# First stage of a two-block transformer kernel: the first value tile moved ahead of modulation tiles 8 and 9, and the tokens' sums of squares moved from VectorE to TensorE

## What is computed

```python
sc_lat, sc_ctx = jax.nn.silu(c), jax.nn.silu(c_ctx)
m_l = (sc_lat @ w_ada[l] + b_ada[l])[:, None, :]
m_c = sc_ctx @ w_ada[l] + b_ada[l]
sh1, sc1, g1, sh2, sc2, g2 = jnp.split(m_l, 6, axis=-1)
csh1, csc1, cg1, csh2, csc2, cg2 = jnp.split(m_c, 6, axis=-1)
hl = modulate(rmsnorm(lat, norm_g[l, 0]), sh1, sc1)
hc = modulate(rmsnorm(cx, norm_g[l, 0]), csh1, csc1)
...
q, zf_fwd, zf_bwd, v, g = jnp.split(h @ w_in, 5, axis=-1)
```

## Time and profile before

| | |
|---|---|
| median of three executions | 931.19 us |
| the profiled execution | 931.22 us, with a span of 929.4 us |
| TensorE (PE) busy | 908.6 us, 98% |
| VectorE (DVE) busy | 647.0 us, 70% |
| ScalarE (ACT) busy | 507.7 us, 55% |
| granted TensorE clock, mean | 0.994 of full speed |
| chain of waits, by engine | PE 91%, DVE 4%, DMA 1%, ACT 1%, issue 1%, SPq 1% |

### The profile page before, as it was taken

How to read it: one execution, slowest core, us unless ns; L and a number is a source line. 1 busy time by engine, 2 the same in 40 slices (tenths; PEclk the granted TensorE clock), 3 DMA queues, 4 the chain that set the end, 5 groups by cost and what they waited for, 6 DMA issues and landing times.

```text
span 929.4 us, 17184 instructions
## 1 busy us (share of the span) xinstructions
PE 908.6 (98%) x6354; PEld 830.5 (89%) x6354; DVE 647.0 (70%) x1054; ACT 507.7 (55%) x798; POOL 0.2 (0%) x4
## 2 busy tenths in 40 slices
PE   7899999999999999999999999999999999999997
PEld 5468888888899999999998998999999899999996
DVE  5978488888887777676677866774466766555555
ACT  6642466666664665555556655544464565444443
POOL 0000000000000000000000000000000000000000
PEclk9899999999999999999999999999999999999999
DMA  9829553443425265655654443344445446555551
GB/s 346 322 104 348 222 191 136 137 135 135 132 95 181 70 210 177 202 176 169 198 182 157 133 159 120 134 173 154 169 146 202 157 159 222 185 181 181 188 185 57
DMA packets 45343, 160.94 MB, mean 173 GB/s; under 512 B 5104, under 2 KB 6512, under 8 KB 45168
## 3 DMA queue, kind: packets, MB, share of 16 engines
q1 hardware_dynamic: 43536, 156.56, 48.8%
q10 hardware_dynamic: 1760, 3.74, 1.1%
HBM read 159.23 MB, written 1.05 MB: 172 GB/s over the span
## 4 chain that ended last, share of the span: by engine, by line
PE 91%; DVE 4%; DMA 1%; ACT 1%; issue 1%; SPq 1%; DVEq 0%; ACTq 0%
PE bank L438 22%; PE bank L440 21%; PE bank L439 21%; PE bank L1166 4%; PE bank L504 4%; PE bank L505 4%; PE bank L506 4%; DMA arena<-in_stream 1%; DVE w_lo L432 1%; PE bank L1227 1%; PE bank L1269 1%; PE bank L1249 1%; PE bank L1265 1%; PE bank L1199 1%; PE bank L1229 1%
## 5 line engine op out<-in xcount | busy, mean ns | idle before, releaser
L432 DVE TENSOR_TENSOR w_lo<-raw,w_hi 128x1024 fp32r<-128x1024 f32 x248 | 299.7, 1222 | 143.5 <-ACT w_hi L421 143.2
L438 PE MATMUL bank<-h_hi,w_hi 128*128 128x256 f32 (+1 forms) x1248 | 373.9, 300 | 1.9 <-DVE h_lo L620 0.6
L440 PE MATMUL bank<-h_hi,w_lo 128*128 128x256 f32 (+1 forms) x1248 | 366.6, 294 | 0.0
L439 PE MATMUL bank<-h_lo,w_hi 128*128 128x256 f32 (+1 forms) x1248 | 365.9, 293 | 0.0
L421 ACT ACTIVATE w_hi<-raw 128x1024 fp32r<-128x1024 f32 x248 | 257.4, 1051 | 99.0 <-PE bank L440 76.8
L438 PEld LDWEIGHTS bank<-h_hi,w_hi 128*128 128x128 f32 x1248 | 234.6, 188 | 12.1 <-issue 3.6
L439 PEld LDWEIGHTS bank<-h_lo,w_hi 128*128 128x128 f32 x1248 | 236.2, 189 | 6.3
L440 PEld LDWEIGHTS bank<-h_hi,w_lo 128*128 128x128 f32 x1248 | 234.7, 188 | 5.9
L438 PE MATMUL bank<-y_hi,w_hi 128*128 128x256 f32 x304 | 86.9, 286 | 0.0
L440 PE MATMUL bank<-y_hi,w_lo 128*128 128x256 f32 x304 | 85.9, 282 | 0.0
L439 PE MATMUL bank<-y_lo,w_hi 128*128 128x256 f32 x304 | 85.4, 281 | 0.0
(11 more groups left out here) (255 smaller groups left out, 1138.1 us busy)
## 6 DMA issues: line engine op xcount, KB each, us to landing
raw<-in_stream SPq DMA_DIRECT2D x248, 512.0 KB, 3.3
arena<-in_ada SPq DMA_DIRECT2D x24, 512.0 KB, 5.3
arena<-in_stream SPq DMA_DIRECT2D x6, 1024.0 KB, 14.3
xres<-in_ada SPq DMA_DIRECT2D x8, 512.0 KB, 3.2
tok<-in_tok SPq DMA_DIRECT2D x4, 512.0 KB, 9.0
con<-in_con ACTq DMA_DIRECT2D x1, 1472.0 KB, 9.5
xres<-in_tok ACTq DMA_DIRECT2D x1, 1024.0 KB, 9.8
out<-arena SPq DMA_DIRECT2D x4, 256.0 KB, 2.0
```

The lines of the kernel that those rows point to most:

```text
L432: dve.tensor_tensor(w_lo[c.slot][:, :], source(c), w_hi[c.slot][:, :].bitcast(F32), ALU.subtract).then_inc(S("split_lo"), 1)
L438: pe.matmul(dst, hi_w, a_hi, start=start, stop=False, skip_group_check=True)
L439: pe.matmul(dst, hi_w, a_lo, start=False, stop=False, skip_group_check=True)
L440: return pe.matmul(dst, lo_w, a_hi, start=False, stop=stop, skip_group_check=True)
```

## The change

On TensorE, value tile 0 becomes chunk 8, directly behind modulation tiles 0 to 7, and modulation tiles 8 to 15 follow it. The seven additions on VectorE and the one product with ones are gone. In their place TensorE multiplies each tile of squares with the matrix of ones itself: eight products that add up in bank 1, two each behind modulation tiles 2, 3, 5 and 7 (`PIECE_BEHIND`). The zero products behind tiles 0 to 3 and 9 are gone (25 of them), and 10 stand ahead of value tile 0 (`FILL`). Loads, ScalarE's and VectorE's instructions are put in an order that goes with this. The core of the diff:

```diff
-TOPPED = (5, 5, 5, 4, 0, 0, 0, 0, 0, 6)
+FILL = 10
+PIECE_BEHIND = (2, 3, 5, 7)
-V_FIRST = KT + AHEAD
+V_FIRST = KT
...
             for i in range(KT):
                 ada(i)
-                warm(TOPPED[i])
-                if i == 3:
-                    pe.wait_ge(S("tok_added"), KT - 1)
-                    pe.matmul(psum[1][:, :], ones, wide[:, 0:TC], start=True, stop=True).then_inc(S("tok_summed"), 1)
+                if i in PIECE_BEHIND:
+                    n = PIECE_BEHIND.index(i)
+                    pe.wait_ge(S("tok_squares"), n + 1)
+                    for k in range(2 * n, 2 * n + 2):
+                        last = pe.matmul(psum[1][:, :], ones, wide[:, k * TC:(k + 1) * TC], start=k == 0, stop=k == KT - 1)
+                    if n == 3:
+                        last.then_inc(S("tok_summed"), 1)
                 if i == 5:
                     turn_rows(0)
             turn_rows(1)
+            warm(FILL)
...
             lo(dve, Chunk(4))
             lo(dve, Chunk(5))
+            quarter(0)
+            lo(dve, Chunk(6))
+            lo(dve, Chunk(7))
+            lo(dve, Chunk(V_FIRST))
+            quarter(1)
             norm_tokens(0)
             norm_tokens(1)
-            lo(dve, Chunk(6))
-            quarter(0)
-            norm_tokens(2)
...
             split_tokens(0)
-            lo(dve, Chunk(V_FIRST))
             split_tokens(1)
             lo(dve, Chunk(V_FIRST + 1))
+            norm_tokens(2)
+            norm_tokens(3)
+            lo(dve, Chunk(V_FIRST + 2))
+            split_tokens(2)
+            lo(dve, Chunk(V_FIRST + 3))
+            split_tokens(3)
             for k in range(4, KT):
                 norm_tokens(k)
-            split_tokens(2)
-            lo(dve, Chunk(V_FIRST + 2))
-            split_tokens(3)
-            for n in range(V_FIRST + 3, EARLY):
+            for n in range(V_FIRST + 4, EARLY):
                 lo(dve, Chunk(n))
             quarter(2)
```

More of the change, by code:

```diff
@@ L118 @@
 WARM = 12
-TOPPED = (5, 5, 5, 4, 0, 0, 0, 0, 0, 6)
-SKIPPED = (4, 3, 2, 3)
+FILL = 10
+PIECE_BEHIND = (2, 3, 5, 7)
+SKIPPED = 3
 E_QD, E_QE, E_KE, E_KD = 1, 4, 5, 6
@@ L417, in hi @@
             else:
-                act.wait_ge(S(f"loaded{c.slot}"), c.round * 16 + (16 - 16 * SKIPPED[c.slot]))
+                act.wait_ge(S(f"loaded{c.slot}"), c.round * 16 + (16 - 16 * SKIPPED))
             if n >= RING:
@@ L699, in load_stream @@
                     load(stream_in, i * (RING * P) + u * P, u)
[L701 to L709, removed]
             def load_ada(pair):
@@ L714, in load_ada, with load_tokens @@
                              stream_in[first:first + 2 * P, :].rearrange("(c p) n -> p c n", p=P)).then_inc(S(f"ada_in{pair}"), 16)
+            def load_tokens(n):
+                x = slice(n * 2 * TC, (n + 1) * 2 * TC)
+                sp.dma_start(tok[:, x], tok_in[:, x]).then_inc(S(f"tok_in{n}"), 16)
             def load_one(n, split):
@@ L718, in load_one @@
                 load(stream_in, n * P, n % RING)
[L720 to L723, removed]
+            sp.dma_start(cc[:, :], cc_in).then_inc(S("cc_in"), 16)
+            load(stream_in, 0, 0)
+            sp.dma_start(con[:, 0:2 * P], con_in[:, 0:2 * P]).then_inc(S("con_in"), 16)
+            load(stream_in, P, 1)
+            load(stream_in, 2 * P, 2)
+            load_tokens(0)
+            load(stream_in, 3 * P, 3)
+            load_tokens(1)
+            sp.dma_start(par[:, :], par_in).then_inc(S("par_in"), 16)
+            load_ada(0)
+            load_tokens(2)
+            load_ada(1)
+            load_tokens(3)
+            load_one(V_FIRST, 1)
+            for pair in range(2, KT - RING // 2):
                 load_ada(pair)
@@ L732, in load_mods @@
                     sp.dma_start(mod_raw[slot], ada_in[n * P:(n + 1) * P, :]).then_inc(S(f"mod_loaded{slot}"), 16)
-            for n, split in ((EARLY, 2), (EARLY + 1, V_FIRST + 1), (EARLY + 2, 4)):
+            for n, split in ((EARLY, 2), (EARLY + 1, 3), (EARLY + 2, 4)):
                 load_one(n, split)
+            sp.wait_ge(S("split_lo"), V_FIRST + 3)
             load_mods(0)
@@ L789, in modulate, with square_pieces @@
                     act.activation(x, x, ACT.Identity, scale=gain[:, k:k + 1], bias=shift[:, k:k + 1]).then_inc(S("modulated"), 1)
-            for n in range(6):
-                hi(act, Chunk(n))
[L793 to L796, removed]
-            copy_rows(0)
+            def square_pieces(n):
+                x = slice(n * 2 * TC, (n + 1) * 2 * TC)
+                act.wait_ge(S(f"tok_in{n}"), 16)
+                act.activation(wide[:, x], tok[:, x], ACT.Square).then_inc(S("tok_squares"), 1)
+            for n in range(3):
+                hi(act, Chunk(n))
+            square_pieces(0)
+            hi(act, Chunk(3))
+            square_pieces(1)
+            hi(act, Chunk(4))
+            hi(act, Chunk(5))
+            copy_rows(0)
+            square_pieces(2)
+            hi(act, Chunk(6))
+            hi(act, Chunk(7))
+            square_pieces(3)
+            act.wait_ge(S("lb_diff"), 1)
+            act.activation(lb_d, lb_d, ACT.Exp).then_inc(S("lb_exp"), 1)
+            hi(act, Chunk(V_FIRST))
+            copy_rows(1)
             act.wait_ge(S("tok_summed"), 1)
@@ L802, in _ @@
             act.activation(rstd, rstd, ACT.Exp, scale=-0.5).then_inc(S("tok_rstd"), 1)
[L803 to L809, removed]
             modulate(0)
-            hi(act, Chunk(V_FIRST))
             modulate(1)
             hi(act, Chunk(V_FIRST + 1))
+            hi(act, Chunk(V_FIRST + 2))
             modulate(2)
-            hi(act, Chunk(V_FIRST + 2))
+            hi(act, Chunk(V_FIRST + 3))
             modulate(3)
-            for n in range(V_FIRST + 3, EARLY):
+            for n in range(V_FIRST + 4, EARLY):
                 hi(act, Chunk(n))
@@ L1610, in split_tokens @@
                 dve.tensor_tensor(h_lo[:, x], tok[:, x], h_hi[:, x].bitcast(F32), ALU.subtract).then_inc(S("h_lo"), 2)
[L1612 to L1619, removed]
             for n in range(4):
                 lo(dve, Chunk(n))
-                add_token_squares(n)
             dve.wait_ge(S("par_in"), 16)
```

2 lines of the change are left out of this document (removed).

## The result

| | before | changed |
|---|---|---|
| median of 20 executions each | 931.38 us | 934.58 us |
| lowest to highest | 929.87 to 933.12 | 932.88 to 935.73 |
| the profiled execution | 931.22 us | 934.72 us |
| start of value tile 1 | 49.45 us | 53.25 us |
| start of value tile 2 | 56.96 us | 60.78 us |

The account below looks back on a forecast made before the run. VectorE was taken to bound the stretch up to value tile 1, behind the loads; 1.7 us for the order plus 0.8 us of low clock gave 2.5, so 931.22 became 933.7 us, own range 932.9 to 935.4, 8-in-10 range 930.6 to 936.2.

Parts of the forecast that it names:

- The bound: From first normalisation to value tile 1's start: VectorE is the bound, busy 24.40 of 26.91 us before the change.
- Loads: Start of the stage: loads land by bytes ahead at 408 GB/s; first pair at 16.1 us, second at 19.9.
- Up to quarter 0: VectorE's lo(4) at 17.15, lo(5) ending at 19.5, and quarter 0's turning on TensorE done at 22.5 us.
- The first normalisation: On VectorE behind piece 3 and rstd: starts at 29.7 us instead of 22.54, 7.2 us later.
- the order alone: Whole path to value tile 1 at full clock: start at 51.15 us, 1.7 us later.
- The rest of VectorE's work: VectorE's normalisations, splits and quarter 2 from 29.7 us until value tile 1 starts at 51.15.
- The clock term: TensorE from tile 11 on: one low-clock stretch of 3.4 us on the path costs 0.8 us, bounds 0 and 2.6.
- the slower rival: Low clock at piece 3 as well, or through tiles 11 to 15: 4.2 us more, 935.4 us; chance 20%.
- the rival at 935.4: Low clock at piece 3 besides tile 11, or through tiles 11 to 15: 4.2 us more; chance 20%.
- The signs: Profile checks: normalisation not before 28, pair of products 1.7 us, VectorE not idle 34 to 49, six value tiles 34.0 us.
- Half-price pieces: TensorE's products with ones: a piece costs 0.86 us, value tile 1 starts at 49.45, total 931.2 us; chance 9%.
- TensorE as the bound: End of the stage: TensorE, not VectorE, sets it; value tile 0 2.2 us earlier gives 929.0 us; chance 10%.

Follow-up runs that it names:

- e1: Changed kernel with VectorE's quarter(0) moved behind lo(6) and lo(7): 931.63 us, ratio 1.0003 to the kernel before.
- e7: e6 with ScalarE's and VectorE's split of chunk 9 put ahead of quarter 1: 930.06 us, ratio 0.9988 to the kernel before.
- e8: Changed kernel with 18 zero products instead of 10 ahead of value tile 0: 935.32 us, ratio 1.0041 to the kernel before.
- e9: e4 with zero products added, eight each behind tiles 2 and 3, five behind quarter 0's turning: 931.43 us, ratio 1.0001 to the kernel before.
- e3: Changed kernel with eight more zero products behind the turning of quarter 0: 933.75 us, ratio 1.0028 to the kernel before.
- e6: e1 with ten zero products behind modulation tile 10: 931.32 us, ratio 1.0001 to the kernel before.
- e5: Kernel before with four pieces behind tiles 0 to 3, replacing the seven additions and the zero products there: 932.27 us, ratio 1.0016.
- e11: e5 with five zero products behind tile 5 and five behind tile 6: 931.85 us, ratio 1.0005 to the kernel before.
- e4: Changed kernel with squares added on VectorE again and one product with ones behind tile 7: 935.28 us, ratio 1.0038 to the kernel before.

## Why the prediction was right, step by step

- **The bound.** Right: VectorE's chain from `rstd` on, not TensorE, sets the start of value tile 1 (e1, e7, e8).
- **Loads.** `hi(4)` started at 16.10 (16.1 predicted), `hi(6)` at 19.94 (19.9). Landing by the bytes ahead is good to 0.1 us in this execution. In others with the same loads the first pair was up to 0.9 us later (`lo(4)` at 18.13 in e9).
- **Up to quarter 0.** VectorE's `lo(4)` at 17.19 (17.15), quarter 0 at 22.79 (22.5). The 0.3 us has three equal parts: piece 2 started at 20.54 instead of 20.45, it took 1.81 us until the next instruction where I took 1.7, and from the start of the turning to quarter 0 it was 0.44 us where I took 0.35.
- **The first normalisation.** 29.7 predicted for full clock, 31.68 measured. Most of the difference is the clock: from the start of tile 7 at 25.82 to the end of piece 3 at 30.27 in the chain of waits it took 4.45 us, where I had 2.7. In e3, with the clock kept, it was 30.16. So the order alone was undersized too: e3 has value tile 1 2.3 us later than before, not 1.7, and the one execution of the changed kernel with a mean granted clock of 1.000 took 933.66 us, not 932.9.
- **The rest of VectorE's work.** From the first normalisation to value tile 1 I had 51.15 - 29.7 = 21.45 us; it took 53.25 - 31.68 = 21.57.
- **The clock term.** This is the step whose place was wrong. I put one low stretch at tile 11, for 0.8 us, as the likeliest, and one at piece 3 only together with it, in the slower rival. The profiled execution has it at piece 3 and, without effect, in value tile 0; ahead of tile 11 the wait was then only 1.27 us and the clock stayed up. The total of +3.8 us at value tile 1 is the 1.7 that I had for the order, 1.75 of low clock at tile 7 and piece 3 (4.45 - 2.7), 0.2 that had built up before tile 7 and 0.1 behind the first normalisation. So this one execution is closer to the rival at 935.4 than to 933.7. The median, 934.58, lies between them. The order with low clock at piece 3 alone would have been 1.7 + 1.7 = 3.4 us, 934.6, and this case was not among mine: that 933.7 came near is in part luck, since 0.8 us in a place where nothing happened stood for 1.75 us in another. The size of 0.8 us was right where such a stretch did occur (0.8 from e1 to e6, 0.9 in e8). The spread of the 20 executions over 2.9 us fits a low stretch that comes in most and not in all: those with a mean granted clock of 0.996 or more took 932.88 to 933.66 us, with one exception at 934.84, and the rest 934.24 to 935.73.
- **The signs.** VectorE had no idle time between 34 and 49, and the six value tiles took 34.00 us, both as stated. Normalisation did not start before 28. A pair of L1195 products took 1.81 us at full clock and 2.85 at low clock until the next instruction, where I had named other than 1.7 as a sign of being wrong. Value tile 0 at 35.04, the wait for `lo(12)` ending at 46.49 and value tile 1 at 53.25 were 1 to 2 us later than I had put them, most of it by the low clock at piece 3.
- **The two rivals for "not slower".** Half-price pieces fall by the row of 1.88 us. TensorE as the bound falls by e8.
- **The rule on idle gaps.** The Trainium skill ("TensorE: Matmul & The Clock Gate", "Why this matters for your kernels") warns of one long idle gap between bursts of matmuls. Here waits of 1.93 and 2.01 us were followed by half clock, so the trace does not agree that such waits are harmless. But the 0.8 us in my sum stood at tile 11, the one place that this rule allows as well, and only the rival at 935.4 had piece 3.

The cause of the loss is shown: moving `quarter(0)` alone in VectorE's program takes back all of it within the interval (e1 against the changed kernel), the low clock at piece 3 with it, since the wait of 1.93 us that preceded it is gone in e1. It is a cause with two parts. VectorE stands at `quarter(0)` because the piece ahead of the turning makes the quarter late, and without the pieces, with the clock kept, the loss is gone as well (e9). The earlier value tile is in e1, e6 and e9, which are all level with the kernel before, so it costs nothing that can be measured; the same holds for the pieces once nothing stands and waits behind them (e1, e6). In the order of the kernel before that is not shown (e5 and e11).

## What to carry to other kernels

When work is moved off an engine, ask what that engine will now stand and wait for: an in-order engine that waits for a small result in front of work whose data are already there gives away the whole lead. In a stretch where several engines hand over to each other, count what the slowest of them still has to do behind the last late input (here `rstd`), and move from behind it whatever does not need it; this was worth 1.3 us in e7 with no instruction saved. Where two changes meet, as the pieces and the place of `quarter(0)` did, undoing either can cure the loss; one experiment on each is needed to see that neither is the cause by itself. Products that seem superfluous can be what keeps TensorE at 2.4 GHz: look at the granted clock behind every wait before removing them, and fill only waits that stand ahead of work on the path.

## What was unexpected of the hardware

- Taking seven of the eight products with ones off TensorE, about 6 us at 0.86 us each by estimate (e4 against the changed kernel), made nothing faster, because the engine then worked at a granted 0.50 for 13.6 us on end. Zero products alone brought 3.9 us back (e9).
- Which of several waits of 1.3 to 2.0 us is followed by half clock differs from case to case: 1.93 us was in the changed kernel, while waits of 1.4 to 1.5 us near 18 us in e3, e6 and e9 were not, and e7's 1.89 us ahead of tile 1 and 1.73 us ahead of value tile 0 were not either. The wait of 2.01 us ahead of value tile 0 was followed by it in e3, e6 and the changed kernel, and not in e1 (1.00 from 30 to 43.7).
- Executions of one kernel on one core differ by 1.4 to 4 us here (e7: 929.62 to 931.05; e5: 930.37 to 934.29) with mean granted clocks of 0.997 and 0.992 in e5; for changes of 0.1% this is what limits the measurement.
